# Expert stage of a two-layer diffusion backbone: full-row weight transfers, both column halves in PSUM, groups in turn, unrolled

## What is computed

```python
def expert_choice_ffn(h, w_router, w_gate, w_up, w_down):
    b, n, d = h.shape
    cap = CAPACITY_FACTOR * n // N_EXPERTS
    logits = jnp.einsum('bnd,de->ben', h, w_router).astype(jnp.float32)
    affinity = jax.nn.softmax(logits, axis=1)
    gates, idx = lax.top_k(affinity, cap)
    xs = jax.vmap(lambda hb, ib: hb[ib])(h, idx)
    a = jnp.einsum('becd,edf->becf', xs, w_gate)
    u = jnp.einsum('becd,edf->becf', xs, w_up)
    y = jnp.einsum('becf,efd->becd', jax.nn.silu(a) * u, w_down) * gates[..., None].astype(h.dtype)
    return jax.vmap(lambda yb, ib: jnp.zeros((n, d), yb.dtype).at[ib.reshape(-1)].add(yb.reshape(-1, d)))(y, idx)
```

## Time and profile before

| what | value |
|---|---|
| median of 3 runs | 2428.0 us |
| the profiled execution's own time | 2422.05 us |
| its span, first to last instruction | 2420.3 us |
| PE busy | 2094.7 us, 87% |
| PE weight loads (beside PE) | 987.8 us, 41% |
| DVE, ACT, POOL busy | 822.4, 503.8, 94.3 us |
| moved by DMA | 504.63 MB, mean 209 GB/s over the span |
| granted TensorE clock, mean | 0.961 of full |

### The profile page before, as it was taken

How to read it: one execution, slowest core, us unless ns; L and a number is a source line. 1 busy time by engine, 2 the same in 40 slices (tenths; PEclk the granted TensorE clock), 3 DMA queues, 4 the chain that set the end, 5 groups by cost and what they waited for, 6 DMA issues and landing times.

```text
span 2420.3 us, 28798 instructions
## 1 busy us (share of the span) xinstructions
PE 2094.7 (87%) x10962; PEld 987.8 (41%) x10962; DVE 822.4 (34%) x2136; ACT 503.8 (21%) x1177; POOL 94.3 (4%) x69
## 2 busy tenths in 40 slices
PE   5999989999838989999999899999994878787976
PEld 3434455656523333333333456466652323232322
DVE  3321365767660120110201432378765001110102
ACT  3200054545321010100100321255441000100000
POOL 1100000000000000000000101000000000000000
PEclk9999999999979999999999999999997999999999
DMA  9774020000057979979889302200004999999995
GB/s 334 292 265 172 1 70 1 1 1 1 1 195 277 373 259 360 358 256 372 309 317 356 129 18 70 70 1 1 1 1 178 367 387 387 387 388 387 387 386 224
DMA packets 238102, 504.63 MB, mean 209 GB/s; under 512 B 11194, under 2 KB 16236, under 8 KB 233500
## 3 DMA queue, kind: packets, MB, share of 16 engines
q1 hardware_dynamic: 233312, 487.00, 55.1%
q0 software_dynamic: 2880, 10.49, 1.2%
q10 hardware_dynamic: 1788, 5.43, 0.6%
HBM read 495.55 MB, written 7.34 MB: 208 GB/s over the span
## 4 chain that ended last, share of the span: by engine, by line
issue 63%; PE 13%; SPq 13%; DMA 6%; DVE 3%; ACT 1%; POOL 0%; POOLq 0%; DVEq 0%; ACTq 0%; PEldq 0%
SPq L377 13%; PE psS L519 9%; DMA arena<-in_w_down 4%; PE psT L519 2%; DMA arena<-in_w_up 1%; DMA arena<-in_w_gate 1%; ACT arena L946 1%; PE psO L519 1%; PE psM L519 1%; DVE idx L1617 0%; DVE arena L1616 0%; DMA arena<-normed_rows,LIU 0%; PE psS L522 0%; DVE arena L1619 0%; DVE X L1671 0%
## 5 line engine op out<-in xcount | busy, mean ns | idle before, releaser
L519 PE MATMUL psS<-arena 128*64 128x512 f32 (+7 forms) x4896 | 1167.1, 565 | 105.2 <-DMA arena<-in_w_down 31.4
L519 PEld LDWEIGHTS psS<-arena 128*64 128x64 f32 (+4 forms) x4896 | 465.7, 154 | 723.8 <-issue 674.3
L519 PE MATMUL psT<-arena 128*64 128x512 f32 (+1 forms) x1536 | 259.9, 595 | 24.2 <-DMA arena<-in_w_up 18.9
L946 ACT ACTIVATE arena<-psS 128x128 f32<-128x128 f32 (+4 forms) x146 | 54.7, 412 | 858.8 <-PE psS L519 824.9
L522 PE MATMUL psT<-ident,arena 128*128 128x128 f32 (+1 forms) x926 | 147.9, 291 | 89.2 <-DVE arena L1527 27.8
L522 PEld LDWEIGHTS psT<-ident,arena 128*128 128x128 f32 (+1 forms) x926 | 106.6, 145 | 170.5 <-issue 88.1
L1513 DVE TENSOR_REDUCE mx<-psS 128x1 f32<-128x768 f32 (+2 forms) x200 | 165.0, 825 | 28.6 <-PE psS L519 27.0
L946 ACT ACTIVATE arena<-psS,nb 128x768 f32<-128x768 f32 (+2 forms) x200 | 159.1, 796 | 71.1 <-DVE nb L1518 69.3
L1679 DVE TENSOR_TENSOR arena<-arena,psS 128x512 f32<-128x512 f32 x16 | 11.0, 688 | 461.9 <-PE psT L519 461.9
L519 PEld LDWEIGHTS psT<-arena 128*64 128x64 f32 (+1 forms) x1536 | 82.1, 123 | 196.7 <-issue 196.7
L519 PE MATMUL psM<-arena 128*128 128x512 f32 x352 | 156.9, 596 | 4.0 <-DVE X L1473 3.0
(11 more groups left out here) (184 smaller groups left out, 1237.6 us busy)
## 6 DMA issues: line engine op xcount, KB each, us to landing
arena<-in_w_gate SPq DMA_DIRECT2D x128, 1024.0 KB, 13.3
arena<-in_w_up SPq DMA_DIRECT2D x128, 1024.0 KB, 12.5
arena<-in_w_down SPq DMA_DIRECT2D x128, 1024.0 KB, 13.6
arena<-in_w_mod SPq DMA_DIRECT2D x34, 1024.0 KB, 6.6
gtb<-in_w_mod SPq DMA_DIRECT2D x14, 1024.0 KB, 6.7
arena<-in_w_in SPq DMA_DIRECT2D x6, 2048.0 KB, 9.2
normed_rows<-arena ACTq DMA_DIRECT2D x10, 512.0 KB, 9.7
arena<-in_w_out SPq DMA_DIRECT2D x8, 512.0 KB, 7.7
```

The lines of the kernel that those rows point to most:

```text
L519: return nc.tensor.matmul(o, lhsT, rhs, start=start, stop=stop)
L946: return nc.scalar.activation(o, i, f, **kw)
```

## The change

It rewrites the expert stage; attention and router keep their code.

- A transfer is now 256 full rows of a matrix (128 partitions x 2 rows x 1024 columns), still 1 MB. A stage is a quarter of a matrix's rows, 12 stages a quad as before.
- Both column halves of a matrix are accumulated at once: block g has banks 2g and 2g + 1, so layer 0 fills banks 0 to 5, and the small jobs have banks 6 and 7 only. Gate's result leaves the banks by ACT's Silu before up's begins.
- PE works in groups (pair, pair, context) in turn within each stage, each group raising `done`. SP waits for the group that read a slot: in layer 1 two slots come free per pair, in layer 0 all four with the context group.
- The ring has 11 slots in layer 0 and 13 in layer 1, filled from the start (`open`).
- Turns of hidden blocks and tokens stand singly between groups, and the combine of quad q stands after stage 0 of quad q + 1; only the last stands alone. High and low parts lie over `HIDT` and `XG`.
- No loop is left; all four quads are straight code. The next gather waits for tokens turned or the combine finished.

```diff
-RSTAGES = (2, 3)
+NSLOT = (11, 13)
...
-                with sp.Fori(0, NQ) as q:
-                    for st in range(12):
-                        m, hf, kh = stage_of(st)
-                        w = A[("w_gate", "w_up", "w_down")[m]][l]
-                        sp.wait_ge(z["wused"], q * 12 + (st + 1))
-                        for e in range(QUAD):
-                            slot = st % RSTAGES[l] * QUAD + e
-                            load(ar[:, RING + slot * SLOT:RING + (slot + 1) * SLOT].rearrange("p (k n) -> p k n", k=4),
-                                 w[bass.ds(q * QUAD + e, 1), kh * 512:(kh + 1) * 512, hf * 512:(hf + 1) * 512]
-                                 .rearrange("e (k p) n -> p (e k) n", p=P), s_w[slot])
+                sp.wait_ge(z["open"], l + 1)
+                for j in range(NLOAD):
+                    if j >= NSLOT[l]:
+                        st, e = divmod(j - NSLOT[l], QUAD)
+                        sp.wait_ge(z["done"], groups_done(l, 0, st, 2 if l == 0 else e // 2))
+                    q, st, e = j // (NSTAGE * QUAD), j // QUAD % NSTAGE, j % QUAD
+                    w, kq, slot = A[("w_gate", "w_up", "w_down")[st // 4]], st % 4, RING + j % NSLOT[l] * SLOT
+                    load(ar[:, slot:slot + SLOT].rearrange("p (k n) -> p k n", k=2),
+                         w[l, q * QUAD + e, kq * 256:(kq + 1) * 256, :].rearrange("(k p) n -> p k n", p=P), s_w[j % NSLOT[l]])
...
+                def combine(q):
+
+                    pe.wait_ge(z["st"], q + 1)
+                    pe.wait_ge(z["yl" if wc else "y"], (q + 1) * NX)
+                    for n, (t, h) in enumerate(CJ):
+                        b = 6 + n % 2
+                        take(b)
...
+                    for h in range(2):
+                        for k in range(2):
+                            for e in experts:
+                                a = src + (2 * kq + k) * W + col + e * n
+                                r = RING + ((q * NSTAGE + st) * QUAD + e) % NSLOT[l] * SLOT + k * D + h * 512
+                                p0 = n * (e - experts[0])
+                                last = mm(bank(2 * g + h, p0, n), ar[:, a:a + n], ar[:, r:r + 512], kq == 0 and k == 0, kq == 3 and k == 1)
+                    last.then_inc(z["done"], 1)
...
+                for x in range(KD):
+                    turn_tokens(0, x)
+                for q in range(NQ):
+                    for st in range(NSTAGE):
+                        for g in range(NX):
+                            if st == 8 and g == 1 and wc:
+                                turn_hidden(q, 2)
+                            group(q, st, g)
+                            if st == 7 and g == 1:
+                                turn_hidden(q, 0)
+                            if st == 7 and g == NX - 1:
+                                turn_hidden(q, 1)
+                            if q < NQ - 1:
+                                for x in turns.get((st, g), ()):
+                                    turn_tokens(q + 1, x)
+                        if st == 0 and q:
+                            combine(q - 1)
+                combine(NQ - 1)
```

More of the change, by code:

```diff
@@ L936, in _, with take, turn_tokens @@
-                with pe.Fori(0, NQ - 1) as q:
-                    quad(q, False)
-                quad(NQ - 1, True)
+                CJ = combine_jobs(tl)
+                turns = TURN_AT if wc else TURN_AT_2
+                free = {6: None, 7: None}
+                def take(b):
+                    if free[b]:
+                        pe.wait_ge(*free[b])
+                def turn_tokens(q, x):
+                    b = x if q == 0 else 6 + x % 2
+                    if q:
+                        take(b)
+                        pe.wait_ge(z["xg"], 16 * NX * (q + 1))
+                    elif x == 6:
+                        pe.wait_ge(z["lgev"], 2 * l + 2)
+                    for i in range(NX):
+                        a = F["XG"] + i * D + x * P
+                        last = tr(bank(b, col=i * P, w=P), ar[:, a:a + P])
+                    last.then_inc(z["gp"], 1)
+                    if b >= 6:
+                        free[b] = (z["gd"], 4 * l + x // 2 + 1) if q == 0 and x % 2 else (z["ge"], x // 2 + 1 if q == 0 else KD * q - 4 + x + 1)
@@ new lines, in combined, with gated @@
+                def combined(q):
+                    for n, (t, h) in enumerate(CJ):
+                        dve.wait_ge(z["cp"], q * len(CJ) + n + 1)
+                        a = t * D + h * 512
+                        V.tensor_tensor(X[:, a:a + 512], X[:, a:a + 512], bank(6 + n % 2), ALU.add).then_inc(z["ce"], 1)
+                def gated(q, g):
+                    dve.wait_ge(z["done"], groups_done(l, q, 7, g))
+                    dve.wait_ge(z["silu"], q * NX + g + 1)
+                    for h in range(2):
+                        a = HID + g * D + h * 512
+                        last = V.tensor_tensor(ar[:, a:a + 512], ar[:, a:a + 512], bank(2 * g + h), ALU.mult)
+                    last.then_inc(z["prod"], 1)
@@ L1712, in _ @@
                                         modcol[:, m + 8:m + 9], ALU.mult, ALU.add)
[L1713 to L1717 removed]
+                    V.tensor_scalar(ar[:, a:a + 256], bank(x, w=256), eff[:, k:k + 1], modcol[:, m:m + 1],
+                                    ALU.mult, ALU.add).then_inc(z["gd"], 1)
@@ new lines, in _ @@
+                for q in range(NQ):
+                    if q:
+                        combined(q - 1)
+                    selection(q)
+                    gated(q, 0)
+                    gated(q, 1)
+                    hidden(q, 0)
+                    if wc:
+                        gated(q, 2)
+                    hidden(q, 1)
+                    if wc:
+                        hidden(q, 2)
+                    for g in range(NX):
+                        weighted(q, g)
+                combined(NQ - 1)
```

353 lines of the change are left out of this document (131 added, 222 removed).

## The result

The changed kernel takes 2354.5 us (median of 4 runs, 2351.3 to 2356.5) against 2430.9 us (2425.5 to 2434.5) for the kernel before, measured beside it. The ratio is 0.9686 with a 95% interval of 0.9662 to 0.9711: **76.4 us less**. Forecast were 2350 us and 78 us less.

A forecast was written before the change was run, and what follows sets the result against it. PE and its gaps were taken to bound layer 0, transfers layer 1. Gains of 40.8 and 37.2 us made 78 us less, 2428 - 78 = 2350 us; range 2334 to 2392.

The forecast's parts named there:

- Layer 0's terms: Layer 0: products 508.8, hidden turns 15.2, token turns 11.4, combines 42.0, last chain 4.4, sum 581.8 us; 40.8 less.
- The start: Layer 0's first group begins right after eight token turns, at 736.4 instead of 738.0, saving 1.6 us.
- the combine: Adding a quad's outputs in layer 0 over two banks takes 10.5 us, four times 42.0.
- The turns: Layer 0's transposes between groups cost only themselves: hidden 3.8 us a quad, tokens 3.8 for each of three quads.
- The last combine's wait: At layer 0's end, weighting, high and low part of the last block stand in a chain, 4.4 us.
- seven slots are ahead: Layer 0's weights keep up: 10.8 us a stage at 387 GB/s against 10.6 of products plus 3 of small jobs.
- One bound: Limit on layer 0's gain: a combine without waits gives 43 us.
- Layer 1's rate: Layer 1's loads in 4 KB pieces run at 413 instead of 387 GB/s, 2.54 us each, worth 30.4 us.
- The tail: Layer 1 from the last landing to the span's end: 32.5 us, before 30.8, as both column halves are weighted last.
- Rival 1: Layer 1's rate stays at 387 GB/s despite 4 KB pieces; total gain 48 us, 2380 us; chance 0.17.
- Rival 2: Single turns and two-bank combines lose 0.3 us per hand-over; layer 0 gains only 17 us, 2374 us; chance 0.13.
- Rival 3: Straight code in both layers starves PE of instructions; slower, up to 2630 us less what layer 1 absorbs; chance 0.05.

## Why the prediction was right, and where it was off

**What bounds each layer** was read rightly. Layer 0 followed PE and layer 1 the transfers, and each edit moved the layer it was meant for: short pieces cost 28.2 us in layer 1 and 0.1 in layer 0.

**Layer 0's terms.** A looping quad was worked out as 127.2 + 3.8 + 3.8 + 10.5 = 145.3 us; it takes 145.4. From the first group (738.81) to PE's end (1322.85) it is 584.0 where the sum said 581.8. The start is as forecast: the first group stands 5.3 us behind the first turn, before it was 6.8. The term that was short is the combine: 11.0 instead of 10.5 for each of three, because the jobs of the context block, which come first, wait for one of two banks, and 12.7 for the last. The turns were priced a little too high and hide part of this. The last combine's wait was right (4.72 against 4.4), but I priced the products behind it at 0.227 us each, and behind this gap PE ran at its lower clock for some 5 us. The rows for that were there: I had used the same effect in favour of the change at the quad's start, and left it out at the one gap that the change creates.

**Which of before's waits these were** came out a little differently. Unrolling alone gave 12.7 us. The other 26.4 came with the rest of the change: PE's waits in layer 0 happen to be 26.4 us too in the unrolled kernel of before, and 6.2 in after. The remaining 6.2 us are mostly less busy time: PE is busy 582.4 us there and 577.9 in after. Single turns are worth 2.1 us a quad and not 3.7, since products that don't read the turned tokens need not wait whichever way the turns stand. The ring of 11 is worth 3.5 us. The prediction had costed it at nothing by averages ("seven slots are ahead"), and it counted 3 us of small jobs a stage where its own terms make 1.5 (18.1 us a quad over 12 stages). A stage of 4.19 MB takes 10.2 us at 409 GB/s and a stage of products 10.6, so by this estimate a ring of 8 has 0.4 us a stage to catch up where no small job stands. One bound was off as well: a combine without waits, 40 products at 0.227 us, would by the prediction's prices have made the gain 46 us and not 43.

**Layer 1's rate** was mis-sized by 1%: 409 GB/s instead of 413. Loads take 2.564 instead of 2.54 us, and 179 x 0.024 = 4.3 us. The `w_out` stretches were 3 us long and read 411 and 416, and I took their middle. The six gathers still to come were put at 6 us, though the same sum had 8.1 for them before; they move 3.15 MB, 7.7 us at 409. SP resumed 7.5 us after the first turn (forecast 7.2). With these the last load lands 523.1 us after the layer's first, 32.7 less than before and not 38.8; 4.3 + 1.7 + 0.3 covers the difference. Counted back from the last landing, the full flow began 3.3 us after SP's issue (forecast 3.4). The tail is 32.3 us (forecast 32.5). By the kernel with pieces of 2 KB the length gave 28.2 us (forecast 30.4) and everything else 3.1 (forecast 6.8).

**The rivals.** Rival 1 would have given 2380 us, and the kernel with pieces of 2 KB, which is just that case, took 2382.4. The Trainium skill, "DMA: Bandwidth & Descriptors", section "Specifications", lets line rate begin at 512 B; here the rate still rose from 387 to 409 and 419 GB/s with pieces of 2, 4 and 8 KB. Its 358 GB/s per core is a memory's rate divided by two cores, and this core, which ran alone, moved more. By the Trainium skill, same page, section "Why small descriptors are slow (HBM only)" 2 to 4 KB is an estimated step from 387 to 396; the trace shows 409. Rival 2 is false: no idle time stands between turns and groups, and the two-bank combines show 1.5 us in all. Rival 3 is false too. PE shows no idle time put down to issue within layer 0's stages, and one of 0.7 us in layer 1, although layer 1's quads now fetch instructions throughout (queue of instructions, layer 1, after: 14 packets in 474 us, before 6). Its premise was half wrong: in layer 0 the looping code had been fetched each time too, 32 packets before against 27 after.

```profile
q8 instruction: 14, 0.23, 0.2%
```

**The total** agrees better than its parts, and that is luck. The two layers gave 70.4 of the forecast 78. The medians differ by 76.4, largely because the one traced execution of before is 8.8 us shorter than its median. Where these 8.8 us lie no trace shows. In the seven runs of before that stand beside the last experiments the shortest, 2422.9 us, has a mean granted clock of 0.962 and the longest, 2431.1, one of 0.956. So some of them may lie in PE's slow products, which would make layer 0's true gain larger.

## What to carry to other kernels

Where the queues are busy all the time, make each piece that a partition receives longer before anything else, and give the layout that this needs to the order in which the other operand is turned. Where PE bounds a stage, small jobs cost only their own time if each stands between products that don't depend on it; and each gap of 4.7 us in this stage cost a further 1 to 2 us afterwards at the lower clock, so a chain that must end the stage should begin with what is ready. Do not take the rate of a stretch of 3 us for that of a long one: here 411 and 416 GB/s became 409.

## What the hardware showed that I had not expected

- The rate still grows beyond 4 KB: 387, 409 and 419 GB/s at 2, 4 and 8 KB. Over the 16 engines that is 84.7, 160 and 313 ns a piece. Doubling 2 KB adds 75.5 ns and not 84.7, so by this estimate about 9 ns of a piece do not depend on its length; the step to 8 KB gives 8.
- A 1 MB transfer split in two of 0.5 MB costs nothing (543.2 us for layer 1 both ways).
- A turn of layer 0's loops costs PE 3.8 us of idle time and 1.3 of slower products, here 5.1 of 160 us. Two packets of instructions move at each turn and none where the same code is written out, which shows 0.91 us of idle time. Straight code fetched fewer packets in layer 0 than the loops (27 against 32).
- After gaps of 4.7 us PE's granted clock is down: 0.50 behind the chain, and 0.65 over the first group after a gather's 7.3 us. Four products on constants in the gap bring it back for the work that counts (1.00 over that group). Behind eight token turns with gaps of up to 1.3 us it was down in two quads of the unrolled kernel and not in the third (5.33, 3.65 and 5.07 us for the same 16 records).
